# A hybrid attention and convolution layer: SP's DMA order in the last pass, and the widening of the reciprocals moved from ScalarE to VectorE

## The reference

```python
h = rmsnorm(x, pre_norm_g[l])
u = h @ w_in[l]
q, k, v, g_att, c_val, c_glu, g_conv = jnp.split(u, split_pts, axis=-1)
a = chunk_attention(q, k, v, rel_bias[l]) * jax.nn.silu(g_att)
c = conformer_conv(c_val, c_glu, dw_w[l], dw_b[l], conv_ln_g[l], conv_ln_b[l],
                   w_pw[l], b_pw[l]) * jax.nn.silu(g_conv)
y = jnp.concatenate([a, c], axis=-1) @ w_out[l]
x = x + rmsnorm(y, post_norm_g[l])
```

## Time and profile before

| | us |
|---|---|
| median of 3 runs (2621.18 to 2632.18) | 2628.39 |
| profiled execution, device time | 2628.39 |
| its span in the profile | 2626.6 |
| PE busy | 2376.9 (90%) |
| PEld busy | 2188.1 (83%) |
| DVE busy | 1662.9 (63%) |
| ACT busy | 977.5 (37%) |
| POOL busy | 289.9 (11%) |

### The profile page before, as it was taken

How to read it: one execution, slowest core, us unless ns; L and a number is a source line. 1 busy time by engine, 2 the same in 40 slices (tenths; PEclk the granted TensorE clock), 3 DMA queues, 4 the chain that set the end, 5 groups by cost and what they waited for, 6 DMA issues and landing times. The chain is left out here.

```text
span 2626.6 us, 45407 instructions
## 1 busy us (share of the span) xinstructions
PE 2376.9 (90%) x16468; PEld 2188.1 (83%) x16468; DVE 1662.9 (63%) x3142; ACT 977.5 (37%) x1835; POOL 289.9 (11%) x260
## 2 busy tenths in 40 slices
PE   5999999999998899999999589994899989989997
PEld 5999999999997888898889367783688888888886
DVE  5756656656656888888887534441566666666665
ACT  4111111111113222212221344441677777777774
POOL 0000000000000000000000000000033233233242
PEclk9999999999998999999999799997799999999998
DMA  5322222222224433233322443226556556556553
GB/s 170 109 93 72 92 93 71 92 94 70 92 97 141 150 142 137 96 133 138 138 99 85 147 110 112 87 109 176 137 147 193 151 143 190 148 144 189 153 131 120
DMA packets 207900, 327.45 MB, mean 125 GB/s; under 512 B 16626, under 2 KB 141562, under 8 KB 207769
## 3 DMA queue, kind: packets, MB, share of 16 engines
q1 hardware_dynamic: 206680, 324.69, 39.9%
q10 hardware_dynamic: 1088, 1.05, 0.2%
HBM read 198.24 MB, written 127.46 MB: 124 GB/s over the span
## 5 line engine op out<-in xcount | busy, mean ns | idle before, releaser
L261 PE MATMUL p_pb<-h_hT_hi,p_w_hi 128*128 128x256 f32 x3072 | 873.8, 284 | 39.6 <-DVE h_hT_lo L204 24.5
L263 PE MATMUL p_pb<-h_hT_hi,p_w_lo 128*128 128x256 f32 x3072 | 864.5, 281 | 0.0
L262 PE MATMUL p_pb<-h_hT_lo,p_w_hi 128*128 128x256 f32 x3072 | 864.4, 281 | 0.0
L261 PEld LDWEIGHTS p_pb<-h_hT_hi,p_w_hi 128*128 128x128 f32 x3072 | 581.5, 189 | 45.3 <-DVE p_st L455 22.6
L262 PEld LDWEIGHTS p_pb<-h_hT_lo,p_w_hi 128*128 128x128 f32 x3072 | 582.3, 190 | 0.7
L263 PEld LDWEIGHTS p_pb<-h_hT_hi,p_w_lo 128*128 128x128 f32 x3072 | 581.5, 189 | 0.0
L638 DVE SCALAR_TENSOR_TENSOR p_acc<-p_hgl,k_dwt,p_acc 128x512 f32<-128x512 f32 x544 | 368.1, 744 | 0.0
L423 DVE SCALAR_TENSOR_TENSOR p_acc<-p_hg,k_dwt,p_acc 128x256 f32<-128x256 f32 x832 | 337.0, 477 | 0.0
L1365 DVE CUSTOM_DVE_ANT_0 p_pr<-p_s,p_bias 128x640 f32<-128x640 f32 (+4 forms) x256 | 198.9, 777 | 156.7 <-PE p_s L1464 153.9
L1270 ACT ACTIVATE p_pr<-p_pr,p_nmax 128x640 f32<-128x640 f32 (+4 forms) x256 | 203.8, 796 | 124.4 <-DVE p_nmax L1365 122.4
L1373 DVE TENSOR_TENSOR p_pt_lo<-p_t,p_pt_hi 128x640 fp32r<-128x640 f32 (+4 forms) x256 | 199.3, 779 | 52.6 <-ACT p_pt_hi L1278 52.6
(11 more groups left out here) (155 smaller groups left out, 3813.0 us busy)
## 6 DMA issues: line engine op xcount, KB each, us to landing
h_x<-in_x SPq DMA_DIRECT2D x32, 1024.0 KB, 6.1
q_parts<-p_st SPq DMA_DIRECT2D x64, 256.0 KB, 2.3
k_parts<-p_st SPq DMA_DIRECT2D x64, 256.0 KB, 2.4
v_parts<-p_vst SPq DMA_DIRECT2D x16, 1024.0 KB, 4.6
y_conv<-p_yst SPq DMA_DIRECT2D x64, 256.0 KB, 2.0
p_ks<-k_parts SPq DMA_DIRECT2D x32, 512.0 KB, 6.9
p_vs<-v_parts SPq DMA_DIRECT2D x16, 1024.0 KB, 9.3
p_y<-y_conv SPq DMA_DIRECT2D x16, 1024.0 KB, 7.8
```

What stands on the lines that cost most here:

```text
L261: nc.tensor.matmul(out, stat_hi(k), mov_hi(k), start=(k == 0), stop=False)
L262: nc.tensor.matmul(out, stat_hi(k), mov_lo(k), start=False, stop=False)
L263: mm = nc.tensor.matmul(out, stat_lo(k), mov_hi(k), start=False, stop=(k == tiles - 1))
```

## The change

Two things change in pass 4, and no arithmetic.

First, SP's order. `end_rows(g)`, which loads `y_conv` of group g, stores group g-1 and loads x of group g, is no longer called in group g+1 after the load of the gate. It stands at the end of group g's body, after the loads of q for group g+1, so that it precedes the loads of k, v and gate of group g+1's body. Its waits are the same.

Second, the widening. `widen` is gone from ACT. DVE's `tail("rec")` now makes both halves of `recx` itself, by two `tensor_scalar` operations, right after the reciprocal, for which it waits. The wait of the reciprocal for `recx_ok` and the one of the widening for `r_ps` are gone.

```diff
@@ sync
                 if not is_first(g):
                     sp.wait_ge(m_read, 6 * (g - 1) + 2)
                     load_ga(g)
-                if not (isinstance(g, int) and g < 2):
-                    end_rows(g - 1)
                 if not is_last(g):
                     for half in range(2):
                         sp.wait_ge(s_ps, 16 * g + 8 * (half + 1))
                         load_q(sp, g + 1, half)
-
-            def end_rows(g):
-                sp.wait_ge(sum_ok, 2 * g)
-                load_yc(g)
-                store(g - 1)
-                sp.wait_ge(x_out, DMA * g)
-                load_x(g)
+                if not is_first(g):
+                    sp.wait_ge(sum_ok, 2 * g)
+                    load_yc(g)
+                    store(g - 1)
+                    sp.wait_ge(x_out, DMA * g)
+                    load_x(g)
 
             all_groups(sp, body)
-            end_rows(NG - 1)
@@ scalar
-            def widen(g):
-                act.wait_ge(rec_ok, g + 1)
-                if not is_first(g):
-                    act.wait_ge(r_ps, 2 * g)
-                for half in range(2):
-                    hs = slice(4 * half, 4 * half + 4)
-                    nc.scalar.activation(recx[:, 2 * half:2 * half + 2, :].rearrange("p t (h d) -> p t h d", d=HEAD_DIM),
-                                         rec[:, :, hs, None].broadcast_to([P, 2, 4, HEAD_DIM]), ACT.Copy, scale=0.5).then_inc(recx_ok, 1)
-
             def body(g, quad, slot):
                 for h in range(HEADS):
-                    if h == 0 and not is_first(g):
-                        widen(g - 1)
                     for t in range(2):
...
             lower(NG - 1, HEADS - 1)
-            widen(NG - 1)
@@ vector
                 if part == "rec":
                     dve.wait_ge(exp_ok, 16 * (g + 1))
-                    if not is_first(g):
-                        dve.wait_ge(recx_ok, 2 * g)
                     nc.vector.reciprocal(rec[:, :, :], psum_[slot % 2][:, :, :]).then_inc(rec_ok, 1)
+                    dve.wait_ge(rec_ok, g + 1)
+                    for half in range(2):
+                        hs = slice(4 * half, 4 * half + 4)
+                        nc.vector.tensor_scalar(recx[:, 2 * half:2 * half + 2, :].rearrange("p t (h d) -> p t h d", d=HEAD_DIM),
+                                                rec[:, :, hs, None].broadcast_to([P, 2, 4, HEAD_DIM]), 0.5, None, ALU.mult).then_inc(recx_ok, 1)
```

## The result

The changed kernel takes 2666.33 us (median of 4 runs, 2659.37 to 2668.94) against 2627.26 us of the kernel before on the same chip: a ratio of 1.0157, 95% interval 1.0136 to 1.0179. That lies above the predicted range.

A forecast was written before the change was run, and what follows sets the result against it. The prediction took PE, busy for 90% of the span, as the bound. Its terms, -9.6 (early `y_conv`) + 8.1 + 2 (widening on DVE) = +0.5 us, gave 2629 us, no change, with a range of 2603 to 2646.

The forecast's parts named there:

- `y_conv` lands in time, -9.6: Output projection: the earlier load removes all PE waits for the add L1404, -9.6 us; bounds 0 and -9.6.
- under 0.5: Sign of being right: the add L1404's wait for the `y_conv` DMA is under 0.5 us.
- x goes out 8.7 us after `y_conv`: SP's queue: the x load, waiting for the store, is issued 8.7 us after `y_conv` where nothing else travels.
- The need for q at 27.6 us: Next group's head 0: scores need q 27.6 us after the issue of `y_conv` in the shortest group.
- q is there 25.0 to 28.6 us after the issue: SP's queue: q arrives 25.0 to 28.6 us after `y_conv`'s issue; cost nothing, bounds 0 and +14 us.
- the transfer behind x: x, k, v, gate and half of q, 4.7 MB at 319 or 256 GB/s: 14.8 to 18.4 us.
- Each `tensor_scalar` pair 0.85 + 2.5 us, POOL before the second: DVE at group start: first near 0.85 us, second near 2.5, held for a whole POOL operation; scores 1.10 us later.
- A: Group start: DVE keeps its turn or never needs POOL's; scores 0.6 us sooner in 12 groups, -7.5; 2609 us, 30%.
- B: Group start: POOL keeps the ports into the next L1242, second widening let in at 2110.0; +37, 2656 us, 11%.
- +8.1 and +2 for part two: Widening on DVE: later scores cost 6.6 us in six groups, 1.5 in six others; more low clock adds 2.
- 0 at the loop's jumps: After the two loop jumps PE is late itself, so the moved widening costs 0 there.
- Rival C: SP's loads: `y_conv` lands as late as before (+9.6), or q 0.7 us late in 14 groups (+10); 2639 us, 17%.

The follow-up runs named there:

- e3: Kernel before with SP's new order, but the store wait and x load behind the next q's first half; widening on ACT: 2613.83 us, ratio 0.9965.
- e13: Changed kernel, in which SP waits for the first half of q to land before issuing the second: 2655.41 us, ratio 1.0115 to the kernel before.
- e8: Changed kernel, in which the load of x brings only 128 of its 1024 columns: 2624.20 us, ratio 0.9992 to the kernel before.
- e1: Kernel before with only SP's new order, the widening staying on ACT: 2647.54 us, ratio 1.0078.
- e4: Changed kernel, in which POOL waits with its gain until both halves are widened: 2671.92 us, ratio 1.0167 to the kernel before.
- e2: Kernel before with only the widening moved to DVE, SP's order as before: 2633.16 us, ratio 1.0030.
- e7: Changed kernel, with the store wait and x load moved behind the next q's first half: 2621.21 us, ratio 0.9981 to the kernel before.
- e5: Changed kernel, with q and gate read from a fixed place in 4 KB rows instead of 1 KB: 2658.19 us, ratio 1.0128 to the kernel before.

## Why the prediction was wrong, step by step

- **`y_conv` lands in time, -9.6: right.** Its wait fell from 32.0 to 7.1 us (0.7 in each of 10, where I had said under 0.5), and PE's at the projection is gone. e3, which keeps this and has q in time, is 9 us faster than the kernel before.
- **x goes out 8.7 us after `y_conv`: right in nine groups**, 8.86 in the one shown; in the other four it is 9.4 to 10.1. **The need for q at 27.6 us: right**, 27.6 to 27.9.
- **q is there 25.0 to 28.6 us after the issue, "I cost it at nothing", bound +14: the step that failed.** It came 29.5 to 32.5 us after it, 32.5 in the group shown. The mis-sized term is the transfer behind x: 14.8 to 18.4 us and 1.5 to start (for which I had no row), 16.3 to 19.9 together, against 20.8 to 23.6. Two things were off. The higher of my two rates was that of a mixture: in the trace before, 2112 to 2117, where k travels, moves 224 GB/s, and 2117.5 to 2124, with `y_conv` and the store, 385. No group came near 319; the lower rate, 256, was nearly right. And I counted 4.7 MB, but 5.0 to 5.6 MB moved; the rest belongs to the second half of q, which SP issues while the first half still travels. In the group shown, 2091 to 2114.5, 5.6 MB moved at 240 GB/s. e13 takes that company away and has 20.4 to 21.7 us, still above my upper end of 19.9. e8 shows that x's bytes alone make q late, with SP's stand as it is. By the ratios the late q costs about 30 us (e1 against e3), where I had nothing; in e1 this leaves a loss of 20 us, net of the -9.6 that the early `y_conv` gives.
- **Each `tensor_scalar` pair 0.85 + 2.5 us, POOL before the second: right.** The pair takes 3.17 us; e4 shows that it is POOL. Rivals A and B are out. (A's -7.5 should read -7.2, 0.6 us in 12 groups, which changes nothing.)
- **+8.1 and +2 for part two: right in sum, not in its terms.** Alone it costs 8 (e2) or 4 us (e7). But PE's wait for `nmax` rose by 17 us, since it is 1.46 to 1.53 us in each of 12 groups; and low clock fell (34 to 14 us in e2) where I had it rise: the six groups with a low clock at their beginning have none any more in e2, and so lose the full time too. That the two errors nearly cancel is luck.
- **0 at the loop's jumps: wrong in the changed kernel.** The spread waits 3.50, 2.09 and 1.59 us for `recx` near them (2177.90, 2231.94, 2386.70); there the first `tensor_scalar` of the pair takes 2.3 to 2.6 us. Against that, PE's 9.3 us of waits at the jumps ("issue") are gone, so no run gives the price of this alone.
- **The 13 us by which both parts together exceed their sum.** On its own the widening brings low clock down by 20 us, and with the new order it doesn't (55 us in e1, 57 in the changed kernel). In the changed kernel 11 of the 13 waits for q end within 1.5 us of the beginning of a low stretch. At half speed 20 us of low clock are, by my estimate, about 10 us of work. The lines below have the same work in the kernel before, e2, e1 and the changed kernel, from the spread in group 1 to the one behind the last group. The widening adds as much idling to PE in either order (11.7 and 11.2 us), but PE's busy time falls by 6.1 us in the old order and rises by 3.2 in the new one. That is 9.3 us, and the whole of what the sum misses in these four traces (8.9 us). That it is the clock fits, but no run changed the clock alone.

```profile
1872.62:2597.16 724.54, 670.00 (x4466) 606.19 (x4466) 476.30 (x942) 520.42 (x1048) 230.07 (x164) 0.98 0.57 154
...
1876.34:2606.44 730.10, 663.91 (x4467) 596.57 (x4466) 521.78 (x973) 505.38 (x1017) 232.48 (x164) 0.99 0.57 153
...
1871.26:2619.83 748.57, 672.96 (x4466) 613.02 (x4466) 476.83 (x942) 520.57 (x1048) 231.04 (x164) 0.96 0.58 149
...
1873.05:2636.11 763.06, 676.21 (x4466) 613.98 (x4466) 521.59 (x973) 506.00 (x1017) 232.59 (x164) 0.96 0.57 146
```

- **Rival C had the mechanism** ("q comes 0.7 us late in 14 groups"), but at a quarter of its size: 3.0 us in 13.

## What to carry to other kernels

Before a load is moved ahead of others in a queue, list what then stands behind it, with the bytes in front of each and the time at which each is needed; a margin of a microsecond or two was no margin here, and one megabyte decided. Take the rate from the slices in which that load travels, not from a stretch that mixes it with faster ones, and count whatever is issued before the last byte has landed. An operation on VectorE beside a busy GpSimd cost its place in turn here: one was held for the rest of a GpSimd operation, the second of two in a row for a whole one. Look at more than one group before a number is called typical: the group shown here was the worst of 13.

## What the runs showed of the hardware

- The rule of the Trainium skill on the shared pair of ports (SBUF — State Buffer, section "Who interferes with whom") holds here for a `tensor_scalar` with one float32 source, broadcast: 0.42 us with GpSimd held back, up to 2.63 beside it, and 2.84 with the head as innermost index (0.67 alone).
- A waiting GpSimd is let in between two `tensor_scalar` that follow one another on VectorE: its own operation keeps 2.35 us, and the pair takes 3.17.
- DMAs of one queue overlap at their ends, and need not land in the order of their issue: in the changed kernel the trace has a part of q's second half, issued at 2108.83, landed 4.5 us later, at 2113.3, and the last part of the first half, issued at 2101.65, landed only after 12.6 us, at 2114.3. (Which landing belongs to which of several DMAs with one semaphore is inferred.)
- Issuing two loads of q on SP took 1.29 us, but 3.94 and 4.55 right behind the loads of x, k, v and gate; in e3 it did so too (3.14 and 4.77) and cost nothing. With q in rows of 4 KB it took only 1.16 and 1.24 us at the same place (e5).
